# First modulation and first projections of a fused two-block kernel: from two halves of K to four quarters

## The chip, the cores and the metric

The kernel runs on 1 core of one Trainium2 chip. The metric is the device time of that core in microseconds, as the median of several runs; lower is better. Three runs of the kernel before gave 962.71, 962.02 and 963.41 us.

## The reference, cut to what matters

Two blocks work on one sequence of 256 tokens with 1,024 features. The change is in the first 70 us or so, the start of the first block:

```python
c_act = jax.nn.silu(c)
mod = (c_act @ w_mod[l] + b_mod[l])[:, None, :]
sh1, sc1, g1, sh2, sc2, g2 = jnp.split(mod, N_MOD, axis=-1)
h = rms_norm(x) * (1.0 + sc1) + sh1
proj = h @ w_in[l]
u, v, z, xbc, dt_raw, gate_a, gate_b = jnp.split(proj, offs, axis=-1)
y_a = sgu_branch(u, v, gm_norm_w[l], gm_ws[l], gm_bs[l])
...
```

`sgu_branch` takes `gelu(v)`, normalises it over its features, mixes the tokens of a group of 128 with a matrix per head, and multiplies by `gelu(u)`. `dt_raw` (32 columns) goes through a softplus and feeds a state space branch. Everything that depends on `h` (all of `proj`) needs the shift and scale vectors `sh1` and `sc1`, 2,048 of the 6,144 columns of `mod`.

## The kernel before

**Layout.** Features lie on the partitions: `xres` is x in 8 row tiles (k) of 128 features by 256 tokens. Every weight matrix is cut on the host into panels of 128 x 1024 floats (512 KB): two row tiles by 512 columns. The loop over panels is the same everywhere: SyncE (SP) loads a panel into one of four slots of `raw`; ScalarE (ACT) rounds it to `w_hi` (`split_hi`, line 446); VectorE (DVE) computes the rest, `w_lo = raw - w_hi` (`split_lo`, line 881), and counts the semaphore `taken`, which also lets SP load the slot again; TensorE (PE) multiplies hi by hi, hi by lo and lo by hi (`panel`, lines 1522 to 1524, and `token_panel`, lines 1557 to 1559, where the tokens are the output's partitions) and counts `used`, for which the next `split_hi` of that slot waits. Each engine has its own program, written out by hand, and runs it in order; only semaphores tie them together.

**Start of the first block.** The order of the DMAs on SP is written out by hand: the small tables (`cols`), the 128 KB of dt weights (`wdt`), x in two DMAs, then `load_mod(0, ...)` (8 DMAs of 512 KB), four weight panels, `load_mod(1, ...)`, and more panels. ACT squares x (line 469), PE sums the squares (line 1599), ACT takes the root (line 513, with its table load), DVE inverts it (line 995) into `diag`, the root row.

**First modulation.** `sh1` and `sc1` are one row times a matrix of 1024 x 2048. It is done in two halves of the columns: half 0 holds the 512 columns of shift and the 512 of scale that row tiles 0 to 3 of h need, half 1 those of row tiles 4 to 7. For each of the 8 row tiles of w_mod, DVE multiplies a 128 x 1024 panel by silu(c) of that tile and adds it to `mod_acc` (lines 891 and 893); then PE sums over the partitions by 8 matmuls with one output column each (`mod_sum`, line 1585). In half 0 the first two row tiles (`PE_MOD`) are done by PE instead (line 1605), 8 such matmuls each, and PE fills its waits with matmuls that nobody reads (`keep_warm`, line 1593). DVE adds the bias (line 911).

**Norm.** `first_norm(half)` forms, for 4 row tiles, `tmp_a = x * scale * diag` (line 937), ACT adds the shift and rounds to `act_hi` (line 497), DVE forms `act_lo` (line 942).

**First projections.** In each half PE runs six panels over the 4 row tiles that are ready: two for each of the two 512-column chunks of v (token panels) and two for the first chunk of u. Both chunks of v stay in `proj_ps`, the chunk of u in `aux[:, 2:4]`. In half 1 the dt columns follow in pieces (`dt_part`, lines 1620 to 1622). `mod_sum` of half 1 stands between the fifth and the sixth panel of half 0. After that come the second chunk of u (`chunk(GROUP["u"] + 1, 1)`), a small sum for dt (line 1647), the token mix of the SGU branch (line 1654), then the xbc chunks.

**ACT behind the projections.** In this order: gelu of v chunk 0 (`evac_v(0)`, line 524), two splits, `evac_v(1)`, two squares with sums (line 534), a root (line 537), two splits, gelu of u (line 541), exp (545), a split, ln (548), a split, rounding of a (551), exp (553), two splits, gelu of the second u chunk (line 460). Most of these functions need a table load of their own. DVE computes softplus of dt between them (lines 1030 to 1043), a split, then scales v (line 1050). The SGU matmuls wait for `v_ready` (the scaled v) and `wend_ok` (the exp of line 553).

```python
for half in range(2):
    for n in range(N_HALF):
        k0, at_n = 4 * half + 2 * (n % 2), N_HALF * half + n
        if (half, n) == (0, N_HALF - 1):
            pe.wait_ge(S["mod_acc_ok"], 2 * KT - PE_MOD)
            mod_sum(first_cols(1))
```

Of the kernel before, what the change touches and what calls it, by code (L numbers as in the profile page):

```python
# [14 lines left out]
ALU = mybir.AluOpType  # L15
# [6 lines left out]
P = 128  # L22
# [44 lines left out]
FIRST_ORDER = [0, 1, 4, 5, 8, 9, 2, 3, 6, 7, 10, 11]  # L67
PE_MOD = 2
N_HALF = 6
# [41 lines left out]
def two_blocks(nc, panels, x_t, cols_d, square_d, ws_t, bs_rows, wdt_d, wglr_d, wgu_d, rope_d, levels_d, neg_d, out):  # L111
    with ExitStack() as ctx:
# [10 lines left out]
        mod_first = at("mod_first", 72, [N_MOD_FIRST, 1024])  # L123
# [111 lines left out]
        mod_in = [sem(f"mod_in_{n}") for n in range(KT)]  # L235
# [27 lines left out]
        S = {n: sem(n) for line in names.values() for n in line.split()}  # L263
        def col(name, k=0, n=1):
            return cols[:, COL[name] + k:COL[name] + k + n]
# [9 lines left out]
        def _(sp):  # L275
            sp.dma_start(cols[:], cols_d).then_inc(S["cols_in"], 16)
            sp.dma_start(wdt[:], wdt_d).then_inc(S["wdt_in"], 16)
# [3 lines left out]
            def load_mod(half, rs):  # L281
                for r in rs:
                    for a in range(2):
                        dst = mod_first[:, half * KT + 2 * r:half * KT + 2 * r + 2, 512 * a:512 * a + 512]
                        sp.dma_start(dst, panels[(2 * a + half) * SLOTS + r].rearrange("p (k n) -> p k n", k=2)
                                     ).then_inc(mod_in[half * (KT // 2) + r], 16)
# [17 lines left out]
            def load_first(n):  # L304
                if n >= SLOTS:
                    free(n // SLOTS, n % SLOTS)
                sp.dma_start(raw[:, n % SLOTS, :], panels[N_MOD_FIRST + FIRST_ORDER[n]]).then_inc(landed[n % SLOTS], 16)

            load_mod(0, range(4))
            for n in range(SLOTS):  # L310
                load_first(n)
            load_mod(1, range(3))
            for n in range(SLOTS, N_HALF):
                load_first(n)
            load_mod(1, range(3, 4))
            for n in range(N_HALF, 2 * N_HALF):
                load_first(n)
            first_mod = GROUP["zg"] + 2
            with sp.Fori(2 * N_HALF // SLOTS, first_mod - 1) as i:
                for s in range(SLOTS):  # L320
                    load(i, s)
# [119 lines left out]
        def _(act):  # L441
# [67 lines left out]
            act.wait_ge(S["wdt_in"], 16)  # L509
            nc.scalar.copy(wdt_hi[:], wdt[:]).then_inc(S["narrow_hi_ok"], 1)  # L510
# [3 lines left out]
            split_hi(0, 0)  # L514
            split_hi(0, 1)
            norm_hi(0, lambda k: modc[:, k:k + 1], lambda k: None, range(4))
            split_hi(0, 2)
# [1601 lines left out]
```

## Time and profile of the kernel before

| | |
|---|---|
| median of 3 runs | 962.71 us (962.02 to 963.41) |
| the profiled execution's own time | 962.85 us |
| its span | 961.1 us |
| instructions | 19,143 |
| TensorE busy | 938.2 us, 98% of the span |
| VectorE busy | 693.2 us, 72% |
| ScalarE busy | 534.9 us, 56% |
| bytes read from HBM | 173.63 MB |

The span runs from the first to the last instruction of the profiled execution; its own time is 1.75 us longer. Busy time of an engine is the union of its instructions, weight loads of TensorE counted apart. In the page's table of 40 slices of 24 us the granted TensorE clock is full nearly everywhere, and the DMA engines are 90% busy in the first slice and 40 to 70% later. The stretch that the change touches is the first three slices.

### The profile page before, as it was taken

How to read it: one execution, taken by the hardware profiler on the slowest of the kernel's cores; microseconds unless marked ns; L12 is line 12 of the kernel's file. 1: busy time of each engine (PE TensorE's matmuls, PEld its weight loads, DVE VectorE, ACT ScalarE, POOL GpSimd, SP SyncE). 2: the span in 40 equal slices, each digit the busy share in tenths (PEclk: the TensorE clock that was granted, in tenths of full speed). 3: DMA queues.
4: the chain of work that ended last, by engine and by line, in shares of the span. 5: the costliest groups of instructions: out<-in, count | busy, mean ns of one | idle time of the engine just before them, and what ended most of it. 6: DMA issues, size and time to landing. Idle time of an engine off the chain costs nothing.

```text
span 961.1 us, 19143 instructions
## 1 busy us (share of the span) xinstructions
PE 938.2 (98%) x7436; PEld 891.3 (93%) x7436; DVE 693.2 (72%) x911; ACT 534.9 (56%) x722; POOL 144.4 (15%) x117
## 2 busy tenths in 40 slices
PE   8999999998999999999999999999999999999997
PEld 4799999987998899998999999999888999999996
DVE  4947777787899977566666546389977698877653
ACT  4366655554656674355555435467675676666442
POOL 0100000337588603000000002002200000000010
PEclk9999999999999999999999999999999999999999
DMA  9944555567677665544555655445443355565561
GB/s 336 359 165 138 170 176 175 175 224 217 217 224 246 213 212 178 193 146 161 176 175 175 198 182 177 146 139 169 132 132 110 111 175 190 192 188 184 187 197 45
DMA packets 54987, 175.53 MB, mean 183 GB/s; under 512 B 5440, under 2 KB 5840, under 8 KB 54928
## 3 DMA queue, kind: packets, MB, share of 16 engines
q1 hardware_dynamic: 53952, 172.39, 55.1%
q0 software_dynamic: 368, 1.31, 0.4%
q10 hardware_dynamic: 608, 1.00, 0.3%
q8 instruction: 42, 0.69, 0.3%
q14 instruction: 17, 0.14, 0.0%
HBM read 173.63 MB, written 1.05 MB: 182 GB/s over the span
## 4 chain that ended last, share of the span: by engine, by line
PE 76%; DVE 10%; issue 4%; ACT 4%; POOL 3%; DMA 1%; SPq 1%; POOLq 0%; DVEq 0%; ACTq 0%
PE proj_ps L1522 21%; PE proj_ps L1524 21%; PE proj_ps L1523 21%; DVE conv_acc L1084 4%; DVE w_lo L881 3%; ACT w_hi L446 2%; DVE mod_acc L893 1%; PE proj_ps L1557 1%; ACT conv_acc L566 1%; PE proj_ps L1559 1%; PE proj_ps L1558 1%; PE aux L1572 1%; DMA mod_first<-in_panels 1%; PE aux L1585 1%; PE aux L1868 1%
## 5 line engine op out<-in xcount | busy, mean ns | idle before, releaser
L881 DVE TENSOR_TENSOR w_lo<-raw,w_hi 128x1024 fp32r<-128x1024 f32 x276 | 349.9, 1280 | 176.3 <-ACT w_hi L446 175.9
L446 ACT CAST w_hi<-raw 128x1024 fp32r<-128x1024 f32 x276 | 286.0, 1046 | 227.9 <-PE proj_ps L1524 163.2
L1522 PE MATMUL proj_ps<-act_hi,w_hi 128*128 128x256 f32 x1280 | 366.1, 286 | 2.7 <-issue 0.9
L1524 PE MATMUL proj_ps<-act_hi,w_lo 128*128 128x256 f32 x1280 | 362.7, 283 | 0.0
L1523 PE MATMUL proj_ps<-act_lo,w_hi 128*128 128x256 f32 x1280 | 362.6, 283 | 0.0
L1522 PEld LDWEIGHTS proj_ps<-act_hi,w_hi 128*128 128x128 f32 x1280 | 245.9, 192 | 8.6 <-issue 6.7
L1523 PEld LDWEIGHTS proj_ps<-act_lo,w_hi 128*128 128x128 f32 x1280 | 246.1, 192 | 0.7
L1524 PEld LDWEIGHTS proj_ps<-act_hi,w_lo 128*128 128x128 f32 x1280 | 246.0, 192 | 0.0
L1522 PE MATMUL proj_ps<-ff_hi,w_hi 128*128 128x256 f32 x256 | 72.6, 284 | 0.0
L1524 PE MATMUL proj_ps<-ff_hi,w_lo 128*128 128x256 f32 x256 | 72.4, 283 | 0.0
L1523 PE MATMUL proj_ps<-ff_lo,w_hi 128*128 128x256 f32 x256 | 72.4, 283 | 0.0
L413 POOL TENSOR_TENSOR tmp_b<-tmp_b 128x512 f32<-128x512 f32 x4 | 5.2, 1296 | 441.7 <-ACT tmp_b L469 441.7
L1522 PE MATMUL proj_ps<-glu_hi,w_hi 128*128 128x256 f32 x176 | 50.0, 284 | 0.0
L1524 PE MATMUL proj_ps<-glu_hi,w_lo 128*128 128x256 f32 x176 | 49.8, 283 | 0.0
L1523 PE MATMUL proj_ps<-glu_lo,w_hi 128*128 128x256 f32 x176 | 49.8, 283 | 0.0
L1523 PEld LDWEIGHTS proj_ps<-ff_lo,w_hi 128*128 128x128 f32 x256 | 49.1, 192 | 0.0
L1522 PEld LDWEIGHTS proj_ps<-ff_hi,w_hi 128*128 128x128 f32 x256 | 49.1, 192 | 0.0
L1524 PEld LDWEIGHTS proj_ps<-ff_hi,w_lo 128*128 128x128 f32 x256 | 49.1, 192 | 0.0
L893 DVE SCALAR_TENSOR_TENSOR mod_acc<-raw,silu_c,mod_acc 128x1024 f32<-128x1024 f32 x28 | 41.8, 1492 | 1.3 <-DMA raw<-in_panels 1.0
L1084 DVE SCALAR_TENSOR_TENSOR conv_acc<-proj_ps,cols,conv_acc 128x255 f32<-128x255 f32 (+2 forms) x96 | 38.7, 471 | 0.0
L1522 PE MATMUL proj_ps<-yb_hi,w_hi 128*128 128x256 f32 x128 | 36.8, 287 | 1.4 <-DVE w_lo L881 1.4
L1523 PE MATMUL proj_ps<-yb_lo,w_hi 128*128 128x256 f32 x128 | 36.2, 283 | 0.0
(330 smaller groups left out, 1644.7 us busy)
## 6 DMA issues: line engine op xcount, KB each, us to landing
raw<-in_panels SPq DMA_DIRECT2D x308, 512.0 KB, 3.9
mod_first<-in_panels SPq DMA_DIRECT2D x16, 512.0 KB, 10.7
xres<-in_x_t SPq DMA_DIRECT2D x2, 512.0 KB, 6.3
out_t<-tmp_a SPq DMA_DIRECT2D x4, 256.0 KB, 2.2
wst<-in_ws_t POOLq DMA_DIRECT2D x1, 512.0 KB, 3.8
bs_sb<-in_bs_rows POOLq DMA_DIRECT2D x1, 512.0 KB, 4.6
level_sb<-in_levels ACTq DMA_DIRECT2D x1, 512.0 KB, 4.5
cols<-in_cols SPq DMA_DIRECT2D x1, 267.0 KB, 3.2
```

Source lines behind the costliest of these rows:

```text
L446: nc.scalar.copy(w_hi[:, s, :], raw[:, s, :]).then_inc(hi_done, 1)
L566: ins = nc.scalar.activation(acc[:, c % 2, nt], tile_nt, ACT.Identity, bias=b(NT * c + nt), scale=w(NT * c + nt))
L881: tt(out=w_lo[:, s, :], in0=raw[:, s, :], in1=w_hi[:, s, :].bitcast(F32), op=ALU.subtract).then_inc(taken, 1)
L893: stt(out=mod_acc[:], in0=src, scalar=c_k, in1=mod_acc[:], op0=ALU.mult, op1=ALU.add).then_inc(done, 1)
L1084: ins = stt(out=out, in0=behind_nt, scalar=w(NT * c + nt, taps - 1 - back), in1=out, op0=ALU.mult, op1=ALU.add)
L1522: mm(dst, hi, xh, start=first and k == 0 and nt % 2 == 0, stop=False, skip_group_check=True)
L1523: mm(dst, hi, xl, start=False, stop=False, skip_group_check=True)
L1524: ins = mm(dst, lo, xh, start=False, stop=last and k == ks - 1, skip_group_check=True)
L1557: mm(dst, xh, wh, start=first and k == 0, stop=False)
L1558: mm(dst, xh, wl, start=False, stop=False)
L1559: ins = mm(dst, xl, wh, start=False, stop=last and k == 1)
L1572: ins = mm(aux[:, 2, w * TT + t:w * TT + t + 1], sq[:, k, t * P:t * P + P], avg_d[:, 0:1], start=k + w + t == 0, stop=k == KT - 1, skip_gr ...
```

## The change

The columns of shift and scale are cut into four quarters (256 columns of each) instead of two halves, and the stage works quarter by quarter: w_mod's quarter, the modulation of two row tiles, the norm of two row tiles, and three panels (one per chunk of v, one of u) over those two row tiles. TensorE does five row tiles of the first quarter (0, 1, 2, 3, 7) and VectorE three. x is multiplied by the root row ahead of the modulation (`times_root`), so that the norm is one `tensor_scalar` with two scalars; ACT then only copies. The two halves of `mod_acc` take turns. `mod_sum` of the next quarter stands between the two halves of the u panel. The load of the dt weights moves behind the first three panels, the load of the square-root table ahead of the squares; ACT drains the two chunks of v after the tenth and eleventh panel (before: after the eighth and the tenth). Each DMA of w_mod now moves 256 KB in pieces of 1 KB (before: 512 KB in pieces of 2 KB), 32 DMAs instead of 16.

```diff
+QUARTERS = KT // 2
+FIRST_CHUNKS = 3
+N_FIRST = QUARTERS * FIRST_CHUNKS
+MOD_PARTS = [(0, 0), (0, 1), (0, 2), (0, 3), (1, 0), (1, 2), (2, 0), (3, 0)]
+PE_MOD = (0, 1, 2, 3, 7)
...
-            sp.dma_start(wdt[:], wdt_d).then_inc(S["wdt_in"], 16)
...
+                for r in range(KT // 2):
+                    both = panels[q // 2 * SLOTS + r:q // 2 * SLOTS + r + 2 * SLOTS + 1:2 * SLOTS].rearrange("a p (k n) -> a p k n", k=2)
+                    part = both[:, :, :, 256 * (q % 2):256 * (q % 2) + 256]
                     for a in range(2):
+                        sp.dma_start(mod_first[:, q, 2 * r:2 * r + 2, 256 * a:256 * a + 256], part[a]).then_inc(mod_in[mod_part(q, r)], 16)
...
+            for q in range(QUARTERS):
+                load_mod(q)
+                for n in range(FIRST_CHUNKS * q, FIRST_CHUNKS * q + FIRST_CHUNKS):
+                    load_first(n)
+                if q == 0:
+                    sp.dma_start(wdt[:], wdt_d).then_inc(S["wdt_in"], 16)
...
-            pool.wait_ge(landed[3], 16)
+            pool.wait_ge(landed[3], 2 * 16)
             pool.dma_start(square[:], square_d).then_inc(S["early_in"], 16)
-            pool.wait_ge(landed[3], 2 * 16)
+            pool.wait_ge(landed[3], 3 * 16)
...
+            root_table()
             squares(range(KT))
...
+            first_hi(0)
+            for q in range(QUARTERS):
+                for k in (2 * q, 2 * q + 1):
+                    act.wait_ge(S["nrm_t"], k + 1)
+                    nc.scalar.copy(act_hi[:, k], tmp_a[:, k]).then_inc(S["nrm_hi"], 1)
+                first_hi(FIRST_CHUNKS * q + 1)
+                first_hi(FIRST_CHUNKS * q + 2)
...
+                if q < QUARTERS - 1:
+                    first_hi(FIRST_CHUNKS * q + 3)
 
             def evac_v(j):
-                act.wait_ge(used, N_HALF + 2 * j + 2)
+                act.wait_ge(used, N_FIRST - 2 + j)
...
-            split_all(2)
+            split_hi(3, 0)
             evac_v(0)
-            split_hi(3, 0)
             split_hi(3, 1)
             evac_v(1)
+            split_hi(3, 2)
...
+            def times_root(ks):
+                for k in ks:
+                    dve.wait_ge(x_in[k // 4], 16)
+                    step(tt(out=tmp_a[:, k], in0=xres[:, k], in1=flat(diag[:]), op=ALU.mult))
...
+                for k in ks:
+                    ts(out=tmp_a[:, k], in0=tmp_a[:, k], scalar1=modc[:, 8 + k:9 + k], scalar2=modc[:, k:k + 1], op0=ALU.mult,
+                       op1=ALU.add).then_inc(S["nrm_t"], 1)
...
+            times_root((0, 1))
+            mod_quarter(0, mod_by_dve[0])
+            times_root((2, 3))
+            first_norm(0)
+            first_lo(0)
+            first_lo(1)
+            mod_quarter(1, range(2))
+            first_lo(2)
+            mod_quarter(1, range(2, 6))
+            times_root((4, 5))
+            mod_quarter(1, range(6, 8))
+            first_lo(3)
+            first_norm(1)
             dve.wait_ge(S["narrow_hi_ok"], 1)
             tt(out=wdt_lo[:], in0=wdt[:], in1=wdt_hi[:].bitcast(F32), op=ALU.subtract).then_inc(S["narrow_ok"], 1)
...
+            for q in range(2, QUARTERS):
+                n = FIRST_CHUNKS * q
+                first_lo(n - 2)
+                mod_quarter(q, range(4))
+                first_lo(n - 1)
+                if q == 2:
+                    times_root((6, 7))
+                mod_quarter(q, range(4, 8))
+                first_lo(n)
+                first_norm(q)
...
+            for k in PE_MOD:
+                landed_mod(pe, 0, k)
                 for nt, dst in enumerate(first_cols(0)):
...
-            for n in range(1, KT - PE_MOD):
-                pe.wait_ge(S["mod_acc_ok"], n)
-                keep_warm(1)
...
-            keep_warm(2)
+            keep_warm(3)
...
+            for q in range(QUARTERS):
+                n, k0, ends = FIRST_CHUNKS * q, 2 * q, (q == 0, q == QUARTERS - 1)
+                pe.wait_ge(S["nrm_lo"], k0 + 2)
+                token_panel(n // SLOTS, n % SLOTS, 0, k0, *ends)
+                token_panel((n + 1) // SLOTS, (n + 1) % SLOTS, 1, k0, *ends)
+                for half in range(2):
+                    panel((n + 2) // SLOTS, (n + 2) % SLOTS, 0, act_hi, act_lo, k0, *ends, acc=u0_ps, release=half,
+                          nts=(2 * half, 2 * half + 1))
+                    if half == 0 and q < QUARTERS - 1:
+                        pe.wait_ge(S["mod_acc_ok"], KT * (q + 2) - len(PE_MOD))
+                        mod_sum(first_cols(q + 1), at=512 * ((q + 1) % 2))
+                if q == 1:
+                    pe.wait_ge(S["narrow_ok"], 1)
+                if q:
+                    dt_part(range(0 if q == 1 else k0, k0 + 2))
             pe.wait_ge(evac_act, 2)
             chunk(GROUP["u"] + 1, 1)
```

## Rows read from the trace of the kernel before

**Rows 1.** The page, part 1: busy us, share of the span, instructions.
```profile
PE 938.2 (98%) x7436; PEld 891.3 (93%) x7436; DVE 693.2 (72%) x911; ACT 534.9 (56%) x722; POOL 144.4 (15%) x117
```
**Rows 2.** Windows: stretch us, then busy us (instructions) per engine, clock, DMA, GB/s.
```profile
27.50:49.00 21.50, 20.60 (x113) 18.16 (x114) 20.64 (x25) 8.53 (x12) 2.15 (x3) 0.92 0.90 346
49.00:71.00 22.00, 22.00 (x146) 19.97 (x144) 9.04 (x9) 14.61 (x18) 0.00 (x0) 1.00 0.50 170
```
**Rows 3.** Timeline, TensorE: start us, us, what, idle before it and releaser.
```profile
11.72 0.59 PE L1599 MATMUL aux<-tmp_b,avg_d 128*128 128x256 f32 x2
12.67 3.70 PE L1605 MATMUL aux<-silu_c,mod_first 128*128 128x1 f32 x32 [0.35 <-DMA mod_first<-in_panels]
...
27.53 0.50 PE L1557 MATMUL proj_ps<-w_hi,act_hi 128*128 128x512 f32 x1 [0.68 <-DVE act_lo L942]
...
38.86 0.39 PE L1522 MATMUL aux<-act_hi,w_hi 128*128 128x256 f32 x1 [0.16 <-DVE w_lo L881]
...
42.70 1.98 PE L1585 MATMUL aux<-ones,mod_acc 128*128 128x1 f32 x16 [0.71 <-DVE mod_acc L893]
...
48.97 0.40 PE L1557 MATMUL proj_ps<-w_hi,act_hi 128*128 128x512 f32 x1
...
51.71 0.18 PE L1620 MATMUL aux<-wdt_hi,act_hi 128*128 128x32 f32 x1
...
52.97 0.49 PE L1557 MATMUL proj_ps<-w_hi,act_hi 128*128 128x512 f32 x1
```
**Rows 4.** Timeline, VectorE, same columns.
```profile
13.01 1.75 DVE L995 RECIPROCAL diag<-diag 128x256 f32<-128x256 f32 x1 [6.40 <-ACT diag L513]
...
17.77 5.25 DVE L893 SCALAR_TENSOR_TENSOR mod_acc<-mod_first,silu_c,mod_acc 128x1024 f32<-128x1024 f32 x4 [0.45 <-DMA mod_first<-in_panels]
...
25.33 0.16 DVE L911 TENSOR_TENSOR modc<-aux,cols 128x8 f32<-128x8 f32 x1
...
26.59 0.89 DVE L942 SCALAR_TENSOR_TENSOR act_lo<-tmp_a,modc,act_hi 128x256 fp32r<-128x256 f32 x2 [0.18 <-ACT act_hi L497]
```
**Rows 5.** Groups by form, VectorE, 0 to 60 us: busy us, mean ns, idle before.
```profile
L893 DVE SCALAR_TENSOR_TENSOR mod_acc<-mod_first,silu_c,mod_acc 128x1024 f32<-128x1024 f32 x12 | 15.4, 1283 | 0.7 <-DMA mod_first<-in_panels 0.4
L881 DVE TENSOR_TENSOR w_lo<-raw,w_hi 128x1024 fp32r<-128x1024 f32 x12 | 14.2, 1221 | 3.0 <-ACT w_hi L446 2.8
...
L891 DVE TENSOR_SCALAR mod_acc<-mod_first,silu_c 128x1024 f32<-128x1024 f32 x2 | 1.5, 750 | 0.5 <-DMA mod_first<-in_panels 0.5
...
L993 DVE TENSOR_TENSOR wdt_lo<-wdt,wdt_hi 128x256 fp32r<-128x256 f32 x1 | 0.4, 425 | 1.4 <-ACT wdt_hi L510 1.4
```
**Rows 6.** Windows around the two falls of the clock (columns as in rows 2).
```profile
13.80:17.10 3.30, 3.30 (x26) 2.71 (x25) 2.77 (x3) 0.00 (x0) 0.00 (x0) 1.00 1.05 408
17.20:20.50 3.30, 3.30 (x5) 1.07 (x5) 2.78 (x4) 0.00 (x0) 0.00 (x0) 0.50 1.04 420
...
41.10:44.40 3.30, 2.59 (x24) 2.39 (x22) 3.23 (x4) 1.25 (x2) 1.06 (x2) 1.00 0.61 206
44.50:47.80 3.30, 3.30 (x17) 3.30 (x17) 3.08 (x7) 0.91 (x2) 0.82 (x1) 0.50 0.99 394
```
**Rows 7.** Windows, DMA: 1 KB pieces of `wdt`, then 2 KB pieces of w_mod.
```profile
2.95:3.25 0.30, 0.30 (x2) 0.10 (x1) 0.00 (x0) 0.30 (x1) 0.00 (x0) 1.00 1.17 402
...
12.00:18.00 6.00, 5.65 (x37) 4.37 (x36) 4.02 (x4) 0.97 (x2) 0.00 (x0) 0.93 1.06 410
```
**Rows 8.** Timeline and chain: ScalarE and VectorE ahead of the SGU matmuls.
```profile
57.15 1.28 ACT L524 ACT_TABLE_LOAD   x1
...
64.57 1.02 ACT L524 ACTIVATE v_sb<-proj_ps 128x1024 f32<-128x1024 f32 x1
...
77.92 0.26 ACT L548 ACTIVATE dts<-dts 128x64 f32<-128x64 f32 x1
...
81.31 1.42 DVE L1050 TENSOR_SCALAR v_sb<-v_sb,small 128x1024 f32<-128x1024 f32 x2
...
83.32 3.81 PE aux L1654 x32
```

More of the change, by code:

```diff
@@ L234, in two_blocks @@
         landed = [sem(f"landed_{s}") for s in range(SLOTS)]
-        mod_in = [sem(f"mod_in_{n}") for n in range(KT)]
+        mod_in = {part: sem(f"mod_in_{part[0]}_{part[1]}") for part in MOD_PARTS}
         x_in = [sem(f"x_in_{n}") for n in range(2)]
@@ L263, in two_blocks, with mod_part, landed_mod @@
         S = {n: sem(n) for line in names.values() for n in line.split()}
+        def mod_part(q, r):
+            return max(part for part in MOD_PARTS if part <= (q, r))
+        def landed_mod(eng, q, k):
+            part = mod_part(q, k // 2)
+            eng.wait_ge(mod_in[part], 32 * sum(mod_part(q, r) == part for r in range(KT // 2)))
         def col(name, k=0, n=1):
@@ L306, in load_first @@
                     free(n // SLOTS, n % SLOTS)
[L307 to L317, printed above, removed]
+                sp.dma_start(raw[:, n % SLOTS, :], panels[N_MOD_FIRST + SLOTS * (n % FIRST_CHUNKS) + n // FIRST_CHUNKS]).then_inc(landed[n % SLOTS], 16)
+            for q in range(QUARTERS):
[4 more added lines that the diff above has]
+                    sp.dma_start(wdt[:], wdt_d).then_inc(S["wdt_in"], 16)
             first_mod = GROUP["zg"] + 2
-            with sp.Fori(2 * N_HALF // SLOTS, first_mod - 1) as i:
+            with sp.Fori(N_FIRST // SLOTS, first_mod - 1) as i:
                 for s in range(SLOTS):
@@ L508, in _ @@
             nc.scalar.activation(exp_a[:], col("a_log", 0, HEADS), ACT.Exp).then_inc(S["exp_a_ok"], 1)
-            act.wait_ge(S["wdt_in"], 16)
-            nc.scalar.copy(wdt_hi[:], wdt[:]).then_inc(S["narrow_hi_ok"], 1)
+            root_table()
             squares(range(KT))
@@ L995, in _ @@
-            step(nc.vector.reciprocal(flat(diag[:]), flat(diag[:])))
-            for n in range(PE_MOD, KT):
-                mod_first_panel(n)
-            dve.wait_ge(x_in[0], 16)
-            split_lo(0, 0)
-            split_lo(0, 1)
-            def first_norm(half):
-                norm_apply(0, lambda k: modc[:, 8 + k:9 + k], lambda k: modc[:, k:k + 1], lambda k: None,
-                           range(4 * half, 4 * half + 4), flat(diag[:]))
-            mod_first_evac(0)
-            first_norm(0)
@@ L1580, in row_of, with mod_sum, first_cols @@
                 mm(aux[:, 3, 0:T], ones[:], flat(diag[:]), start=True, stop=True).then_inc(S["rs_mm"], 1)
-            def mod_sum(cols_ps, first=True):
+            def mod_sum(cols_ps, first=True, at=0):
                 for nt, dst in enumerate(cols_ps):
-                    ins = mm(dst, mod_acc[:, nt * P:nt * P + P], ones[:, 0:1], start=first, stop=True, skip_group_check=not first)
+                    ins = mm(dst, mod_acc[:, at + nt * P:at + nt * P + P], ones[:, 0:1], start=first, stop=True, skip_group_check=not first)
                 ins.then_inc(S["mod_mm"], 1)
-            def first_cols(half):
-                return [aux[:, 1, n:n + 1] for a in (0, 8) for n in range(a + 4 * half, a + 4 * half + 4)]
+            def first_cols(q):
+                return [aux[:, 1, a + 2 * q + n:a + 2 * q + n + 1] for a in (0, 8) for n in range(2)]
             def keep_warm(n):
```

119 lines of the change are left out of this document (44 added, 75 removed).

## Prediction

> **What bounds the kernel now.** I read the page first: TensorE is busy for 938 of 961 us [rows 1], so a change is worth what it takes from TensorE's idle or slow time, and nothing else. The table of stretches shows where such time is: from 27.5 to 49.0 us TensorE works through the first six panels at a mean clock of 0.92 with 0.9 us idle, VectorE is busy for 20.64 of 21.5 us; from 49 to 71 us TensorE has no idle time and VectorE works 9 us of 22 [rows 2]. TensorE's timeline gives the marks: the first useful panel starts at 27.53 us, released by VectorE (`act_lo`), and the sum for the second half, at 42.70, waits 0.71 us for `mod_acc` [rows 3]. VectorE works nearly without a break from 13.01 us on [rows 4]. So VectorE bounds the first 45 us, TensorE what follows; at 83.32 us, where the SGU matmuls start [rows 8], everything behind them on TensorE is in the same order as before. The question is when they start.
>
> **Prices.** One half panel of modulation has 512 columns in place of 1,024. Between 0.48 us (256 columns, half of the 0.89 with its overlap, [rows 4]) and 1.283 us (1,024) [rows 5] the straight line gives 0.75, with the wait for the previous one 0.78; half of 1.283 is the low bound, 0.64. The first of a quarter (`tensor_scalar`, 0.75 for 1,024 columns) costs about 0.5. A later quarter is 0.52 + 7 x 0.78 = 6.0 us. A root product is 0.425 + 0.04 = 0.46 [rows 5]. A split costs 1.15 back to back (1.221 less the overlap of 0.07). The norm of two row tiles, bias included, took 25.33 to 27.48, 2.15 us [rows 4]; with `tensor_scalar` and a plain copy I take 1.8. On TensorE a token panel takes 48.97 to 51.71, 2.74 us, dt 1.26 us for two row tiles, a u panel about 2.9 [rows 3]; a sum of four columns is half of 1.95, 0.98, and the five row tiles of quarter 0 cost 20 matmuls x 3.70/16 = 4.6 us [rows 3].
> VectorE's work therefore rises. Modulation was 2 x 0.78 + 12 x 1.32 = 17.4 us and becomes 2.1 + 3 x 6.0 = 20.1, the root products add 3.7, the norm saves about 1.4: 5 us more, although TensorE takes three more row tiles of what was half 0. That is the term against the change.
>
> **Start.** The issue of `wdt` leaves SP's queue ahead of x, so x lands perhaps 0.3 us earlier and its mean square ends at 12.0 (before 12.31, [rows 3]); with the root's table loaded already, VectorE's reciprocal starts at 12.55 (13.01). It ends at 14.3, two root products 15.25, three half panels 17.3. TensorE has its 20 matmuls done at 16.4 and waits. `mod_sum` then starts at 17.35. Before, TensorE was released by a landing at 12.67 and VectorE by another at 17.77, two pairs of row tiles (2 x 1.05 MB) later [rows 3, 4], 2.55 us for each; quarter 0 is 2.1 MB, so it is there in time (below). Before, the clock fell at 17.2 [rows 6] after 3.7 us of one-column matmuls; TensorE does 4.6 us of them now, and no `keep_warm` beside them, so I let it fall again: the sum takes 1.8 us, to 19.15. Norm to 21.0, split of the first panel 22.15, so the first token panel starts at 22.3, 5.2 us earlier than 27.53.
>
> **VectorE to the sums.** From 20.95: two splits 2.3, quarter 1's modulation 6.0, a split 1.15, two root products 0.9: 31.3. TensorE has done 2 x 2.74 + 1.45 = 6.9 us by 29.2 and waits **2.1 us**. From 31.3: split 1.15, norm 1.8, dt's low part 0.4, split 1.2 with its wait for ScalarE, modulation 6.0, split 1.15, root products 0.9: 43.9. TensorE starts quarter 1 at 34.3 (norm), has its two and a half panels done at 41.4 and waits **2.5 us**. In the profile before the clock fell at 44.5 behind 0.7 us of idle and 1.8 us of one-column matmuls, and cost 3.4 us at half speed, 1.6 us of work [rows 6]; here 2.5 us of idle and 1.0 us of such matmuls stand at the same place, so I keep the fall: 43.9 + 0.98 + 1.45 + 2.6 (dt of four row tiles) + 1.6 = 50.5 for the end of quarter 1. From here TensorE is the later one (VectorE has quarter 3's sum ready at 55.85, TensorE asks at 57.3). Quarter 2 is 2 x 2.74 + 2.85 + 0.98 + 1.3 = 10.5, to 61.0; token panel nine (counting from 0) ends at **63.9**; the second u chunk starts at 70.6, where it was 71.04. Of 5.2 us gained at the start, 0.4 is left.
>
> **What is late next.** ScalarE. Before, it drained v chunk 0 at 57.15, between two splits with idle time around; now it waits for ten panels. From `evac_v(1)` at 64.57 to the end of ln at 78.18 it ran 13.6 us with 0.35 idle, and scaled v was ready at 82.73, 4.55 us behind ln [rows 8]. The same list now has a table load, a drain and a split in front, 1.28 + 1.03 + 0.95, less 0.25 of overlap: 16.25 us. So v is ready at 63.9 + 16.25 + 4.55 = **84.7**. TensorE is through with the u chunk at 82.3 and waits 2.3 us; before it started at 83.32. The term is +1.4 us. What follows is in the same order, and I let it carry to the end. Costed at nothing: the moved `wdt` (wanted at 34 us, lands near 20, hidden by raw panels), its round on ScalarE (ScalarE idles there), the table and bias loads on GpSimd's queue, now behind raw panels 7 and 11 (wanted at 82 us, there by 60; if that cover went, the load of 1 MB is 2.6 us), and SP's 16 further issues (eight took 8.1 us with the queue full, the DMA engines stayed full).
>
> **DMA pieces.** Pieces of 1 KB moved 402 GB/s at a busy share of 1.17, pieces of 2 KB 410 at 1.06 [rows 7]: 344 against 387 per full share, so a quarter of 2.1 MB takes 5.8 us in place of 5.1. Quarter 0 lands by 15.3 (VectorE wants its last row tile at 16.5), quarter 1's two parts by 22.3 and 25.2 (wanted 23.2 and 27.2). That costs nothing, with 0.9 us to spare. I take 344, as it is the only row with pieces of this size; at 387 nothing changes either, and what a lower rate costs is a rival below.
>
> Sum against the profiled execution: 962.85 + 1.4 = 964.25, which stands 0.14 above the median of the runs, so **964.2 us**. A measurement of this kernel tells 0.2%, 1.9 us, from no change; this is inside it.
>
> **Rivals.**
> *Faster (0.17).* The half panels cost 0.64 + 0.04 and the clock does not fall at 44: VectorE's two stretches shorten by 0.8 us each, TensorE's waits with them, and 1.6 us is not lost. The tenth panel then ends 3.3 us earlier, at 60.6, and SGU starts at 81.3: 960.8 or a little lower. For it: half panels may overlap more than the row of 1,024 shows. Against it: whole panels paid their 0.04 us gap each time and TensorE still idles about 2 us ahead of the sum.
> *Slower by a third fall of the clock (0.38, with the next).* TensorE idles 2.3 us before the SGU matmuls. If the clock falls behind that as it fell at 44.5, 3.4 us run at half speed in a stretch where TensorE bounds: +1.6, 965.8. It decides where the clock falls behind 2.3 us of idle time alone; at 42 us, before, there was 0.7 us of idle and the one-column matmuls helped. An earlier fall too (at 14 us instead of 17, as less than 2 us of real matmuls stands ahead) makes the 4.6 us of one-column matmuls slower: +0.8, 966.6. The Trainium skill (TensorE: Matmul & The Clock Gate, HAM oscillation) tells of a kernel in which each wait between short bursts makes the next burst start at the slow clock; by that rule each of the three waits here is followed by a fall, and the time is the 965.8 of this rival, since behind the first wait TensorE has 2.5 us to spare. [rows 6] show one such fall, and none behind the 0.7 us at 27 us [rows 3].
> *DMA late (inside the slower chance, 0.08).* If 1 KB pieces from rows 2 KB apart move at 290 GB/s, a quarter takes 7.2 us, quarter 1 lands at 28 instead of 25.2 and its last four row tiles wait about 1: with quarter 0 later by 1.2 us too, +1.5, 965.7. The Trainium skill (DMA: Bandwidth & Descriptors, Rules for kernel authors) wants 1 MiB or more per DMA; the change halves 512 KB to 256 KB. In this trace 512 KB transfers in flow ran at 410 GB/s [rows 7], so size alone does not show. By the same page's fit (Anatomy of one DMA, about 2.0 us and the bytes at 436 GB/s) the eight of a quarter, one after another, would take an estimated 21 us, and the start would be some 40 us longer; by it a pair of the old ones takes 6.4 us, where the rows show 2.55.
> *It doesn't do what it says (0.02):* TensorE's start not earlier than 26 us, because `mod_sum` and three `keep_warm` stand in its queue at half clock. Then VectorE still sets the 31.3, and the result is the main case.
>
> **How the numbers follow.** Main case 0.45, its own range 963.0 to 965.2 (the landing of x by 0.4, the price of a half panel by 0.02 on 14 of them). Faster cases, the clock not falling at 44 with full prices (962.7) among the same: the range begins at 961.0. Slower cases: it ends at 967.0. Chances: faster than 960.8 0.17; within 1.9 us 0.45; slower than 964.6 0.38.
>
> **What would show it.** In the changed profile: the first token panel at 22 to 23 us; TensorE idle 2 us before the sums at 31 and 44, none before the last; a window of clock 0.5 behind 44; the first drain of v at 64; the second u chunk at 70 to 71; idle time of about 2 us before line 1654's matmuls, released by VectorE's scaling of v; those matmuls at 84 to 85. I am wrong if they start before 82 (VectorE's prices or the clock), or if ScalarE is idle between the first drain of v and ln, which would take the tail's term away.

## The result and the profile after

The changed kernel took **968.73 us** (median of 4 runs, 967.67 to 969.32), the kernel before beside it 962.37 (4 runs). The ratio is 1.0057 with a 95% interval of 1.0037 to 1.0077: slower by 5.5 us by the ratio (6.4 by the two medians), and 968.73 is above the predicted range of 961.0 to 967.0. A repeat on another chip (e12, below) gave 1.0047 (1.003 to 1.0064). The profiled execution took 968.55 us, its span is 966.8.

From the page, the line of busy times and the clock's line in 40 slices: TensorE's busy time is 5.4 us above [rows 1], and the clock's line has a 7, two 8s (the third slice, 48 to 72 us, and the tenth) where before it had 9s throughout. The core's mean granted clock is 0.982, before it was 0.994. By stretches of half a microsecond, TensorE stood at half clock for 30.7 us in all (10.2 from 13.7 on, 10.2 from 44.5, 6.8 from 222, 3.4 from 720); before it was 10.2 us, in three falls of 3.4 near 17, 44 and 222.

```profile
PE 943.6 (98%) x7436; PEld 899.0 (93%) x7436; DVE 698.2 (72%) x934; ACT 533.5 (55%) x723; POOL 142.1 (15%) x117
PEclk7989999998999999999999999999999999999999
```

A TensorE that is busy for longer with the same work has worked at a lower clock. The marks, from its timeline:

| mark, us | before | predicted | after |
|---|---|---|---|
| first token panel | 27.53 | 22.3 | 22.77 |
| sum of quarter 1, wait ahead of it | | 31.3, 2.1 | 30.70, none |
| sum of quarter 2, wait ahead of it | | 43.9, 2.5 | 43.38, 2.26 |
| half clock behind 44 lasts | 3.4 | 3.4 | 10.2 |
| quarter 1's work ends, dt with it | | 50.5 | 51.8 |
| token panel 9 ends | | 63.9 | 66.6 |
| second u chunk starts | 71.04 | 70.6 | 73.46 |
| idle ahead of the SGU | 0.38 | 2.3 | 1.82 |
| SGU starts | 83.32 | 84.7 | 87.18 |
| wait in the xbc chunks | 110.16 | | 114.01 |

The first fall, too, lasted 10.2 us instead of 3.4. It covers the three `keep_warm` matmuls behind the first sum, and these, not VectorE (which had the first panel's low part ready by 21.5), held the first token panel until 22.77:

```profile
18.29 5.47 PE L1629 MATMUL aux<-warm,ones 128*128 128x512 f32 x6
22.77 1.41 PE L1593 MATMUL proj_ps<-w_hi,act_hi 128*128 128x512 f32 x1
```

Up to quarter 2's sum this cost nothing, since VectorE sets that sum: it used up the 2.1 us of waiting that was forecast ahead of quarter 1's. The stretches around 44 us (columns: busy us and count of each engine, granted clock, DMA share, GB/s), to be read beside [rows 6]:

```profile
41.10:44.40 3.30, 1.04 (x10) 1.02 (x10) 3.19 (x4) 0.00 (x0) 0.00 (x0) 1.00 1.09 381
44.50:47.80 3.30, 3.30 (x18) 3.30 (x17) 2.61 (x7) 2.66 (x5) 0.00 (x0) 0.50 1.02 391
47.90:51.20 3.30, 3.30 (x17) 3.30 (x17) 3.16 (x6) 0.81 (x1) 0.00 (x0) 0.50 0.57 175
51.30:54.70 3.40, 3.40 (x11) 2.82 (x11) 3.29 (x5) 0.00 (x0) 1.06 (x2) 0.50 0.38 107
54.80:58.10 3.30, 3.30 (x16) 2.67 (x16) 1.54 (x2) 0.00 (x0) 0.00 (x0) 1.00 0.89 302
```

Three stretches in a row stand at 0.50 (1.2 GHz) where before there was one, and TensorE is busy in all of them. What it did there, from its timeline: the wait and the one-column sum, half a u panel, dt's 24 short matmuls (first and last shown), the first token panel of quarter 2:

```profile
43.38 1.05 PE L1621 MATMUL aux<-ones,mod_acc 128*128 128x1 f32 x8 [2.26 <-DVE mod_acc L910]
...
46.81 0.23 PE L1653 MATMUL aux<-wdt_hi,act_hi 128*128 128x32 f32 x1
...
51.57 0.37 PE L1655 MATMUL aux<-wdt_hi,act_lo 128*128 128x32 f32 x1
51.78 0.77 PE L1593 MATMUL proj_ps<-w_hi,act_hi 128*128 128x512 f32 x1
```

dt ran from 46.81 to 51.78, 5.0 us; at full clock the same 24 take 2.6. The end of the tail, on VectorE and TensorE:

```profile
84.33 1.22 DVE L897 TENSOR_TENSOR w_lo<-raw,w_hi 128x1024 fp32r<-128x1024 f32 x1
85.47 0.16 DVE L1084 RECIPROCAL small<-small 128x2 f32<-128x2 f32 x1
85.66 1.42 DVE L1086 TENSOR_SCALAR v_sb<-v_sb,small 128x1024 f32<-128x1024 f32 x2
```

```profile
PE aux L1621 <- DVE mod_acc L910: 2.3, 1, 2.3
PE aux L1686 <- DVE v_sb L1086: 1.8, 1, 1.8
```

From the SGU's start, 3.86 us late, the two traces run side by side for long (the same waits begin at 110.16 and 114.01, 293.19 and 297.20, 438.98 and 443.09). Then the difference grows once more, from 4.1 us to 5.7, in unchanged code of the second block (the next common wait begins at 726.10 and 731.80). TensorE's timeline around it and the clock in the stretches:

```profile
716.60 1.84 PE L1985 MATMUL proj_ps<-avg_v,og 128*128 128x1 f32 x16
718.37 1.13 PE L1927 MATMUL aux<-k_sb,q_sb 64*128 64x256 f32 x4
719.43 0.66 PE L1936 MATMUL aux<-square,prob 128*128 128x128 f32 x4
719.84 0.47 PE L1593 MATMUL proj_ps<-w_hi,act_hi 128*128 128x512 f32 x1
```

```profile
716.90:720.30 3.40, 3.40 (x24) 2.96 (x25) 2.96 (x4) 2.73 (x4) 0.00 (x0) 1.00 0.30 89
720.40:723.70 3.30, 3.30 (x9) 2.63 (x8) 2.07 (x5) 2.68 (x6) 0.00 (x0) 0.50 0.67 215
```

Before, the same work ran at full clock in every stretch from 716 to 723 us. So the 5.7 us between the two profiled executions are 3.9 up to the SGU, 0.2 in between and 1.6 at 720.

### The profile page after: what moved, and what is told of

It is laid out like the page before. It is cut to its first block, busy times and chain, and to the rows that moved or that the text cites. A ratio compares the mean times of both kernels' runs of the same rounds, so it can differ in the third digit from the quotient of the medians.

```text
span 966.8 us, 19203 instructions
## 1 busy us (share of the span) xinstructions
PE 943.6 (98%) x7436; PEld 899.0 (93%) x7436; DVE 698.2 (72%) x934; ACT 533.5 (55%) x723; POOL 142.1 (15%) x117
## 4 chain that ended last, share of the span: by engine, by line
PE 76%; DVE 10%; ACT 5%; issue 5%; POOL 3%; POOLq 0%; DVEq 0%; ACTq 0%
PE proj_ps L1558 21%; PE proj_ps L1559 20%; PE proj_ps L1560 20%; DVE conv_acc L1120 4%; DVE w_lo L897 3%; ACT w_hi L455 2%; PE proj_ps L1593 1%; PE proj_ps L1595 1%; PE proj_ps L1594 1%; PE aux L1621 1%; ACT conv_acc L582 1%; DVE mod_acc L910 1%; PE aux L1608 1%; POOL a_upto_lo L385 1%; PE aux L1900 1%
## 5 line engine op out<-in xcount | busy, mean ns | idle before, releaser
L1560 PE MATMUL proj_ps<-yb_hi,w_lo 128*128 128x256 f32 x128 | 36.2, 283 | 0.0
```

Source lines behind the costliest of these rows:

```text
L1560: ins = mm(dst, lo, xh, start=False, stop=last and k == ks - 1, skip_group_check=True)
```

## The experiments

**Theory.** The fall of the clock behind 44 us lasts three times as long as forecast, since the sum and 24 short matmuls of dt stand around it; the ScalarE tail gives the rest; the fall at 720 follows from where the later work now lies in time. **Rivals:** VectorE's added work is the cost and the clock only goes with it; or the late fall belongs to changed code. The runs were made in four groups, each with its own runs of the kernel before (medians 963.40, 963.32, 964.11 and 963.70); compare ratios rather than medians across groups.

**e1: dt's matmuls moved out of the half-speed stretch.**

```diff
                 token_panel(n // SLOTS, n % SLOTS, 0, k0, *ends)
+                if q == 2:
+                    dt_part((0, 1))
                 token_panel((n + 1) // SLOTS, (n + 1) % SLOTS, 1, k0, *ends)
+                if q == 2:
+                    dt_part((2, 3))
...
-                if q:
-                    dt_part(range(0 if q == 1 else k0, k0 + 2))
+                if q > 1:
+                    dt_part(range(k0, k0 + 2))
```

> The changed kernel with the dt matmuls of row tiles 0 to 3 moved from behind the second quarter (24 short ones in a row, right behind the 2.3 us wait for the sum) to two places in the third quarter, behind its token panels. Theory (the clock): in the changed kernel the clock was at half from 44.5 to 54.8 us, 10.2 us where the kernel before had 3.4, because the wait, the one-column sum and then these short matmuls follow each other. With long matmuls behind the sum it is at half for 3.4 us only: the second u chunk starts 3.4 us earlier (70.0 in place of 73.5), the SGU matmuls at about 83.8, the time is 3.4 us less than the changed kernel's or, if the new fall at 720 us goes too, 5 us. Rival (VectorE and ScalarE alone set it, the clock is a symptom): SGU matmuls at 87, less than 0.7 us of change.

966.25 us (8 runs), ratio 1.0015 (1.0001 to 1.003). In its profile there was no fall near 44 at all, although TensorE waited 2.25 us there as before; the second u chunk started at 69.27 and the idle time before the SGU was again 1.8 us, but the clock fell behind that idle time; the SGU started at 83.00 (83.8 forecast), and the longer fall at 222 and the one near 720 were there too (first row: busy us of five engines, then the clock; second: the SGU's matmuls, 3.8 us in other runs):

```profile
83.70:87.00 3.30, 3.30 (x17) 3.30 (x17) 3.30 (x6) 2.51 (x3) 0.00 (x0) 0.50 0.66 223
```

```profile
L1689 PE MATMUL aux<-wst,v_sb 128*128 128x128 f32 x32 | 5.4, 348 | 1.8 <-DVE v_sb L1086 1.8
```

**e2: three matmuls of 512 columns fill TensorE's wait ahead of quarter 2's sum.**

```diff
+                        if q == 1:
+                            keep_warm(3, 0)
                         pe.wait_ge(S["mod_acc_ok"], KT * (q + 2) - len(PE_MOD))
```

> The changed kernel with three 512-column matmuls that nobody reads (2.6 us) ahead of the wait for the third sum, the place of the 2.3 us wait. Clock theory: no fall at 44.5, the matmuls cost 0.1 to 0.3 us over the wait, 5.1 us of lost work come back: second u chunk at 68.6, SGU matmuls at about 82.3, time 5 us less than the changed kernel's. If the dt matmuls can bring a fall by themselves, it comes 3.4 us later and 1.7 to 3.4 us of the gain are missing. Rival (VectorE sets the sums): the wait is only filled, nothing moves by more than 0.7 us.

964.15 us (10 runs), ratio 1.0001 (0.9992 to 1.0011): nearly all of the 0.57% is gone with one added call. TensorE is busy through the wait, which costs nothing since the sum starts at 43.39 as before, and dt runs at full clock (45.7 to 48.3):

```profile
41.10:44.40 3.30, 3.30 (x15) 1.94 (x14) 3.19 (x5) 0.00 (x0) 0.00 (x0) 1.00 1.08 374
44.50:47.80 3.30, 3.30 (x32) 3.30 (x30) 2.60 (x6) 2.74 (x5) 0.00 (x0) 1.00 0.94 363
47.90:49.30 1.40, 1.40 (x9) 1.24 (x10) 1.33 (x4) 0.84 (x1) 0.00 (x0) 1.00 0.32 73
49.40:52.70 3.30, 3.30 (x10) 2.53 (x9) 3.19 (x5) 0.00 (x0) 0.18 (x1) 0.50 0.38 144
```

A fall of 3.4 us is left, in the token panel behind dt, as the expectation allowed for. The SGU started at 84.07, later than the 82.3 forecast, with 1.82 us of idle time before it, and this profile has no fall at 720.

**e3: both edits.**

> Both edits together. Clock theory: clock at full from 24 us to 220 us, SGU matmuls at 82 to 82.5, bound by ScalarE's chain from its first drain of v; time 5 to 6.5 us less than the changed kernel's, 962 to 963.5, level with the kernel before. Rival: as the changed kernel less 0.7 us at most.

964.22 us (10 runs), ratio 1.0006 (0.9996 to 1.0016), no better than e2. The forecast (full clock from 24 us on, the SGU at 82 to 82.5, 962 to 963.5) was missed: the clock fell for 3.4 us at 31.3, behind 1.2 us of idle time and quarter 1's sum, and quarter 2's sum started at 44.06 instead of 43.39 in e2; then the clock stayed full up to 219 us. The SGU started at 83.71 with 1.82 us of idle time before it.

**e4: fewer function tables in the tail.** exp and ln of dt's softplus become copies times zero; dt is then the positive part of its input.

```diff
-            nc.scalar.activation(dts[:, 5], dts[:, 4], ACT.Exp, scale=-1.0)
+            nc.scalar.activation(dts[:, 5], dts[:, 4], ACT.Copy, scale=0.0)
...
-            nc.scalar.activation(dts[:, 7], dts[:, 6], ACT.Ln)
+            nc.scalar.activation(dts[:, 7], dts[:, 6], ACT.Copy, scale=0.0)
```

> The changed kernel with the exp and the ln of dt's softplus left out (a copy with scale 0 in their place, so softplus becomes max(x, 0)): two table loads of 1.28 us less on ScalarE between the drain of u and dt. Theory of the tail: ScalarE's chain from the first drain of v sets the SGU matmuls, TensorE idles 1.8 us in front of them, so they start 1.8 us earlier (85.4) and the time is 1.8 us less. Rival (the 1.8 us of idle time is bound by VectorE's own queue or made up later): the idle stays above 1 us, or the time does not move.

966.81 us (6 runs), ratio 1.0023 (0.9999 to 1.0046). The idle time before the SGU went from 1.82 to 0.38, as the tail's theory says, but in this profile the half-speed stretch at 44 was 13.7 us long and the SGU started at 87.30: on the changed kernel the clock's scatter hides the term (forecast: the SGU at 85.4, 1.8 us less time). So it was repeated on e3's clock, as **e8**:

> e3's kernel (dt spread, filling matmuls) with the exp and the ln of dt's softplus replaced by copies times zero, so that ScalarE loads fewer tables: dt is then the positive part of its input, not the softplus. Theory (ScalarE's tables and the chain through dt make the 1.8 us before the SGU, and this is the rest of what the change costs once the clock is held): the idle before the SGU falls to 0.4 us or less and the time by 1.4 to 1.8 us under e3, to about 962.5. Rival (that idle hides nothing of later): the median stays at 964.2 within 0.5.

963.42 us (10 runs), ratio 1.0001 (0.9992 to 1.001): 0.8 under e3 by the medians of two groups, 0.5 by the ratios, which the runs do not resolve from nothing (forecast 1.4 to 1.8). In the profile the SGU started at 81.69 with 0.38 us of idle time, 2.0 us before e3's: 1.4 of them are idle time, the rest comes from e3's fall at 31, which this profile doesn't have. The 2.0 us were still there at the xbc wait (108.54 against 110.54); then a fall at 715.5 that e3's profile did not have took 1.6 back. The tail's term is real up to the SGU; that the whole time falls with it is not shown.

**e5: the cause put into the kernel before.** dt of row tiles 0 to 3 moved to right behind the one-column sum at 42.7; nothing added.

```diff
                         mod_sum(first_cols(1))
+                        pe.wait_ge(S["narrow_ok"], 1)
+                        dt_part((0, 1, 2, 3))
...
-                    if half == 1:
-                        dt_part(((0, 1), (2, 3), (4,), (5,), (6,), (7,))[n])
+                    if half == 1 and n > 1:
+                        dt_part(((4,), (5,), (6,), (7,))[n - 2])
```

> The kernel BEFORE with one edit: dt's matmuls of row tiles 0 to 3 (24 matmuls of 32 columns), which stood behind the first two token panels of the second half, stand right behind the one-column sum that follows TensorE's wait at 42.7 (they replace nothing, TensorE does the same work). Theory (a run of sum and short dt matmuls behind a wait is what makes the fall of the clock long in the changed kernel, 10.24 us instead of 3.41): here too the half-speed stretch that begins near 44.5 lasts 6.8 us or more instead of 3.41, the 24 matmuls take about 5 us instead of 2.6, and the second half begins 1.5 to 2.5 us later apart from the 2.6 us moved; median near 964 (963 to 965.5). Rival (the long fall comes from the earlier 2.3 us wait and the two half panels alone, dt only happens to lie in it): the stretch stays at 3.41 us, dt takes about 2.6 us and the median is within 0.5 us of the kernel before.

966.73 us (4 runs), ratio 1.0041 (1.0026 to 1.0057). None of the change's parts is in this kernel, and it loses 3.4 us by the medians (3.9 by the ratio), 2.9 more than the rival allowed and above the theory's 963 to 965.5. The stretches, busy us of five engines and the clock:

```profile
40.90:44.10 3.20, 2.49 (x22) 2.29 (x22) 3.17 (x3) 1.38 (x2) 1.06 (x2) 1.00 0.46 129
44.30:47.60 3.30, 3.30 (x17) 3.30 (x17) 3.08 (x8) 1.42 (x3) 0.75 (x1) 0.50 0.96 360
47.70:51.00 3.30, 3.30 (x17) 3.30 (x17) 3.12 (x5) 1.44 (x2) 0.24 (x1) 0.50 0.37 149
51.10:54.40 3.30, 3.30 (x17) 3.30 (x17) 0.45 (x1) 0.00 (x0) 0.00 (x0) 0.50 0.76 235
54.50:57.80 3.30, 3.30 (x16) 2.68 (x16) 1.23 (x1) 1.49 (x2) 0.00 (x0) 1.00 0.20 77
```

10.2 us at half clock, as in the changed kernel, with only 0.71 us of wait in front. The SGU started at 85.89 instead of 83.32, although the sum at its start came 0.5 us earlier than before (42.19 against 42.70): 3.1 us more from the sum on. This execution is the shortest of the four (964.78), so its marks show the least of the loss. The rival (the long wait and the half panels alone) falls.

**e6: the kernel before, later by one matmul.** 384 columns ahead of the first xbc chunk.

```diff
                 pe.wait_ge(evac_act, EVAC_XBC - 1 + c)
+                if c == 0:
+                    mm(proj_ps[:, 0, 0:384], ones[:], warm[:, 0:384], start=True, stop=True)
                 chunk(GROUP["xbc"] + c, c)
```

> The kernel BEFORE with one added matmul of 384 columns (0.64 us at full clock by the 0.86 us of the 512-column ones) into the bank that the first xbc chunk overwrites, ahead of that chunk: all that follows starts 0.6 us later and is otherwise the same. Theory (the longer half-speed stretch near 222 and the new one near 720 in the changed kernel are consequences of where the later work now falls, not of the changed code): one or both of them appear here as well, and the time grows by more than the 0.6 us added, by 1.5 to 4 us (964 to 966.5). Rival (they belong to what the change did): one stretch of 3.41 us at 222, none at 720, and 962.4 plus 0.0 to 0.7 us.

964.05 us (10 runs), ratio 1.0013 (1.0001 to 1.0024): 0.7 us by the medians and 1.2 by the ratio for 0.64 added, less than the theory asked for; the median does not tell more than the added work. The profile has the second block's fall, in a kernel without any of the change's parts:

```profile
712.50:715.80 3.30, 3.30 (x23) 2.86 (x23) 2.87 (x4) 2.63 (x4) 0.00 (x0) 1.00 0.36 99
715.90:719.20 3.30, 3.30 (x9) 2.58 (x8) 2.07 (x5) 2.66 (x6) 0.00 (x0) 0.50 0.63 209
```

From 438.57 to 727.26, wait to wait, it took 288.7 us; the kernel before took 287.1. The fall at 222 stayed at 3.4 us, so the changed kernel's longer one (6.8 us, from 222.0) was not reproduced this way; it matters little, as the traces of the kernel before and the changed one draw apart by only 0.16 us there. So the fall does not need the change's code. That the shift of 0.64 us brought it is not shown: the changed kernel itself has it in one profiled execution and not in the other (e12), and the kernel before was profiled once, at a mean granted clock of 0.994, while of its 27 runs beside e6, at 0.988 to 0.994, 19 stand at 0.991 or below and so spent more time at half clock somewhere.

**e7: the tail's order, on e3.** VectorE scales v as soon as its root is there, in the time in which it waits for dt's exp, and the SGU's first two groups do not wait for the decay's exp, whose bank they do not write.

```diff
+            dve.wait_ge(S["v_rt"], 1)
+            step(nc.vector.reciprocal(small[:, 4:6], small[:, 2:4]))
+            for t in range(TT):
+                ts(out=v_sb[:, t], ...).then_inc(S["v_ready"], 1)
             dve.wait_ge(S["dt_exp"], 1)
...
-            pe.wait_ge(S["wend_ok"], 1)
             for g in range(GROUPS_SGU):
+                if g == 2:
+                    pe.wait_ge(S["wend_ok"], 1)
```

> The changed kernel with dt spread and the three filling matmuls ahead of the third quarter's sum wait (as e3), and in the tail the scaling of v by its root moved on VectorE from behind dt's softplus to ahead of it (VectorE is idle there for 4.8 us), and the SGU's first matmuls, which write bank 0, no longer waiting for the decay's exp (bank 1). Theory (the tail's last wait before the SGU is the VectorE and ScalarE chain of exp, ln, exp, and of these v's scaling is last): the idle of 1.8 us before the SGU shrinks to 0.5 us or less, the SGU starts near 82.2 instead of 83.7, and the median is 962 to 963.3, 1.0 to 1.8 us under e3 and about level with the kernel before. Rival (what is gained before the SGU is waited for again behind it, at the xbc chunks' panels or the SGU's drain): idle before the SGU is gone but the chunk at 110.5 comes at the same time, and the median equals e3's 964.2 within 0.4.

**961.79 us** (11 runs), ratio 0.9982 (0.9972 to 0.9991): faster than the kernel before by 1.5 us, and 0.2 under the theory's range (2.3 under e3 by the ratios, where 1.0 to 1.8 was forecast). The SGU started at 81.21, 2.5 us before e3's and with no idle time. The two halves of the edit were not run apart. v is scaled at 71.4 to 72.9 instead of 82.2 to 83.6 in e3, and between 60 and 115 us TensorE waits once only, at the xbc chunks:

```profile
71.43 1.42 DVE L1073 TENSOR_SCALAR v_sb<-v_sb,small 128x1024 f32<-128x1024 f32 x2
76.07 0.19 DVE L1076 TENSOR_SCALAR dts<-dts 128x64 f32<-128x64 f32 x1 [3.23 <-ACT dts L561]
```

```profile
PE proj_ps L1557 <- DVE conv_acc L1119: 0.8, 1, 0.8
```

**e9: the same tail edit on the kernel before.**

> The kernel BEFORE with the tail's edit of e7 alone (v scaled ahead of dt's softplus on VectorE; the SGU's first two groups don't wait for the decay's exp). Question: how much of e7's 961.8 is the tail's edit, and does the staged start add anything of its own. Theory (before, the idle ahead of the SGU was 0.38 us and ScalarE's exp ended it, so the edit can win that 0.4 us and no more): 962.3 to 963.3 by the runs' level of before (963.3), idle ahead of the SGU 0.0, and e7 stays faster by some 0.5 to 1 us. Rival (the edit is worth more, since the work behind the SGU comes free too): level with e7 at 961.8.

963.05 us (12 runs), ratio 0.999 (0.998 to 1.0): 1 us, on the edge of what the runs resolve, where 0.4 at most was forecast. e7's ratio is 0.8 us lower; the two intervals overlap, so this pair alone does not show that the quarters add something of their own. e10, with one more edit and in the same group of runs as e9, is 2.2 us under it.

**e10: VectorE's wait for the first sum filled,** on e7.

```diff
-            first_norm(0)
             first_lo(0)
+            first_norm(0)
             first_lo(1)
```

> e7 with the low split of the first weight panel (1.2 us on VectorE) moved ahead of the first quarter's bias add, into the 1.24 us in which VectorE waits for the first one-column sum. Theory (from the first sum to the third quarter VectorE is never idle and sets TensorE's waits): sums 1 to 3 and all behind them come 0.9 to 1.2 us earlier, the median is 960.6 to 961.2. Rival (TensorE's own order is the bound once the filling matmuls stand there, or the later stages wait for something else): first marks earlier, SGU start within 0.3 us of e7's, and a median within 0.4 us of e7's 961.8.

**960.83 us** (8 runs), ratio 0.9973 (0.9963 to 0.9983), the fastest of all, 2.6 us under the kernel before by the ratio (3.3 by the medians of this group) and 2.2 under e9. The median is within the forecast (960.6 to 961.2), the marks are not: 0.9 to 1.2 us earlier was forecast, 0.5 came. VectorE no longer stops at the first sum (in the changed kernel `[1.20 <-PE aux L1621]`):

```profile
16.55 0.88 DVE L1022 TENSOR_TENSOR tmp_a<-xres,diag 128x256 f32<-128x256 f32 x2
17.47 1.23 DVE L897 TENSOR_TENSOR w_lo<-raw,w_hi 128x1024 fp32r<-128x1024 f32 x1
18.61 0.15 DVE L932 TENSOR_TENSOR modc<-aux,cols 128x4 f32<-128x4 f32 x1
...
20.95 1.22 DVE L897 TENSOR_TENSOR w_lo<-raw,w_hi 128x1024 fp32r<-128x1024 f32 x1 [0.51 <-ACT w_hi L455]
```

Half of the gain is lost in the last row, where the second split now waits 0.51 us for ScalarE: quarter 1's bias add came at 31.31 instead of 31.78, and the SGU at 80.73 instead of 81.21. The median fell by more than these 0.5 us, and the profiles differ in a fall near 714 that e7's has and e10's has not.

**e11: one filling matmul among those of the first quarter,** on e10.

```diff
             for k in PE_MOD:
+                if k == 3:
+                    keep_warm(1)
                 landed_mod(pe, 0, k)
```

> e10 with one filling matmul of 512 columns ahead of the fourth of the row tiles that TensorE multiplies in the first quarter. Theory (there TensorE runs only one-column matmuls and keep_warm behind them, and the clock stands at half for 6.8 to 10.2 us from 13.7 to 15.8 on; the sum takes 1.84 us at half and 1.0 us at full clock): the half-speed stretch becomes shorter or starts later, the first sum takes about 1.0 us instead of 1.84 and the bias add is 0.5 to 0.8 us earlier; median 0.3 to 0.8 us under e10. Rival (one matmul of 0.86 us doesn't hold the clock, or it delays the sum by as much as it gives): marks as in e10 or up to 0.9 us later, median within 0.4 us of it.

962.90 us (11 runs), ratio 0.9982 (0.9973 to 0.9992), 2 us worse than e10, which neither the theory nor the rival (within 0.4) allowed. It did not hold the clock (10.2 us at half, from 14.6; e10's profile had 6.8 from 14.4), and its own time delayed the sum, to 18.05 from 16.57; its profile also has a fall near 714, and e10's has not:

```profile
14.70:24.80 10.10, 10.10 (x32) 7.14 (x30) 8.12 (x15) 4.01 (x7) 0.00 (x0) 0.50 1.05 391
```

**e12: the changed kernel again.**

> The changed kernel itself, unaltered, on another chip and in more runs: a control for the size of the loss, since the first comparison had four runs of each. Theory (the half-speed stretch that begins near 44 runs through the half u panel and dt's 24 short matmuls each time): a half-speed stretch of at least 6.8 us that covers dt here too, and a median 3.5 to 6.5 us over the kernel before. Rival (the long fall and the 968.7 were the luck of the first runs): dt takes some 2.6 us at full clock in this profile, and the median is within 2.5 us of the kernel before.

968.75 us (6 runs), ratio 1.0047 (1.003 to 1.0064), as the theory had it. dt of four row tiles took 5.1 us, and the stretches from 44.1 to 57.6 all stand at 0.50 in this profile:

```profile
44.10:47.40 3.30, 3.30 (x17) 3.30 (x17) 2.52 (x6) 1.30 (x3) 0.00 (x0) 0.50 1.06 378
...
54.30:57.60 3.30, 3.30 (x9) 2.54 (x8) 2.93 (x4) 0.00 (x0) 0.00 (x0) 0.50 0.90 326
```

The SGU started at 89.17, 5.85 us later than before. There is no fall at 720: from 445.85 to 732.97, between the two waits used above, this execution took 287.1 us, as the kernel before. So here all but 1.0 us of the difference to the profile of before arose ahead of the SGU.

## Why the prediction was wrong

**What held.** The prices: a half panel took 0.75 to 0.77 us each (three in 2.33), the first of a quarter 0.48, the root products 0.89 for two, and the norm ended near where it was put. The first token panel came 0.5 us late, quarter 2's sum 0.5 early, the wait ahead of it was 2.26 against 2.5. The tail was right in kind and size: v was ready 20.5 us behind token panel 9 (20.8 forecast), TensorE idle for 1.82 us against 2.3, ended by the scaling of v; e8 and e7 took it away and moved the SGU by 2.0 and 2.5 us. Without the clock's surprises the forecast's main case is what runs: e2, with one 3.4 us fall left, had its second u chunk at 70.34 (70.6 forecast) and the SGU at 84.07 (84.7), and gave 1.0001 of the kernel before, against a predicted 1.0015.

**What failed: the step "fall of the clock behind 44".** The prediction kept the old fall, 3.4 us at half clock costing 1.6 of work. It measured 10.2 us (13.7 in two other profiles), or 5.1 us of work: 3.5 more than the term. TensorE waited for nothing more up to the end of the u chunk (VectorE had its part of quarter 3 ready at 55.1), so the loss stayed: token panel 9 ended 2.7 us behind its forecast, after a sum that had come 0.5 early, and the SGU started 2.5 us behind. The prediction looked at what stands ahead of the fall (wait and sum) and not at what stands inside it. Before, that was a u panel of matmuls of 256 columns, then a token panel [rows 3]; here it was half a panel and 24 matmuls of 32 columns. e5 shows that the place of these 24 alone makes the difference, in a kernel with a third of the wait, and e2 that the same 24 run at full clock when the wait ahead of them is filled. All kernels but the changed one were profiled once each; why the chip kept the clock down through this work no run shows.

The first fall was forecast at the sum and priced for the sum alone (1.8 us, to the 1.84 measured); that it would last 10.2 us, through the three `keep_warm` matmuls, was not. It is why the first token panel came 0.5 late (the cause that the prediction named under its chance of 0.02, there with a start at 26 us), and it cost nothing further on.

**What was missing: later falls.** The prediction had no term for falls in unchanged code. The fall at 720 cost 1.6 us in the profiled execution, and e6 shows it in a kernel without the change. It comes and goes between executions and kernels (e2, e3 and the changed kernel's second profile, e12, did not show it; e1, e6, e7, e8 and e11 did), so it is a scatter of one 1.6 us step; whether a shift of the program makes it likelier is open. The loss of the median does not need it: e12's profiled execution took 969.74 us without it. That all of the 5.5 us come from the fall behind 44 and the tail is shown for the marks up to the SGU and, by e2, for nearly all of the median; the division 3.9 + 0.2 + 1.6 holds for the one profiled execution.

**The rivals.** "A third fall" was right about the mechanism and wrong about the place and size: the clock did fall at the SGU in e1, behind the idle time, at the price named (SGU 5.4 us against 3.8), but not in the changed kernel. The section cited there from the Trainium skill (TensorE: Matmul & The Clock Gate, HAM oscillation) tells of a slow start behind each wait of a kernel whose waits are about 3 to 5 us. The waits here are shorter, and a fall followed some of them: it came behind the 2.25 us at 41 in three of four profiles (the changed kernel twice and e4, not e1), behind the 1.82 us before the SGU in one of five. "DMA late" is out: in the stretch in which the first quarter's pieces of 1 KB arrive the DMA engines moved 402 GB/s at a share of 1.08, 372 per full share, better than the 344 that the prediction worked with, and neither TensorE nor VectorE has a wait for `mod_first` between 5 and 60 us. The fit that the prediction quotes there is given by the Trainium skill (DMA: Bandwidth & Descriptors, Anatomy of one DMA) for DMAs issued by GpSimd; the ones here are issued by SyncE.

```profile
8.50:14.50 6.00, 6.00 (x43) 5.72 (x41) 2.75 (x4) 1.47 (x5) 0.00 (x0) 0.94 1.08 402
```

The range should have priced the fall's length from both sides: with 10 us of short matmuls and half panels behind 44, up to three times 1.6 was open. That puts the case at some 967.5, which is above the range given and still 1.2 under the measured median.

## What to carry to other kernels

Where a change bunches short matmuls (a few columns each) near a wait of TensorE, price the half-clock stretch by what runs inside it, not by the length of the last one seen; and keep such matmuls between wide panels, or fill the wait ahead of them, which cost nothing in e2, where VectorE sets the wait's end. A start that is 5 us earlier can be worth nothing if the same engine bounds the next 40 us and a third one the tail: here it paid only after the clock was held and VectorE's idle places in the tail and at the first sum were used. When two kernels differ by less than 1%, look for falls of the clock far away from the edit before explaining the difference by the edit.

## What the runs showed that was not expected

- 24 matmuls of 32 columns took 5.0 us at half clock (the changed kernel) and 2.6 at full clock (e2), and TensorE was busy in every stretch in which the clock stayed down (e5, 44.3 to 54.4).
- One filling matmul of 512 columns among 20 one-column ones (40 in the profile's count) didn't keep the clock up (e11); three in the place of a 2.3 us wait did, up to the end of dt (e2).
- Two profiled executions of the same changed kernel differ by a 3.4 us fall at 720, which cost 1.6 us (in the first, not in e12), and by 3.4 us more at half clock behind 44 (in e12).
- A stretch filled mostly with DMAs of 256 KB in pieces of 1 KB moved 402 GB/s, near the 410 of the old 512 KB ones [rows 7].
